# Latent attention with the values stationary, two heads beside each other in the array, and probabilities normalised before they are turned

## The reference

```
q_nope = rms_norm(q[..., :MLA_NOPE], q_nope_norm)
q_pe = apply_rope(rms_norm(q[..., MLA_NOPE:], q_pe_norm), cos, sin)
k_nope = rms_norm(kv[..., :MLA_NOPE], k_nope_norm)
v = kv[..., MLA_NOPE:]
scale = (MLA_NOPE + MLA_ROPE) ** -0.5
...
    s = (einsum('bqhd,bkhd->bhqk', q_nope, k_nope) + einsum('bqhr,bkr->bhqk', q_pe, k_pe)) * scale
    p = softmax(where(causal_mask(s0, Q_BLOCK, L), s, NEG_INF), axis=-1)
    outs.append(einsum('bhqk,bkhd->bqhd', p, v[:, :L]))
o = concatenate(outs, axis=1)
return o.reshape(B, S, H * MLA_V) @ w_o
```

## Time and profile before

| | |
|---|---|
| median of 3 runs | 1319.57 us (1318.76 to 1322.76) |
| profiled execution, its own time | 1321.25 us |
| its span, first to last instruction | 1319.2 us |
| instructions | 15173 |
| mean granted TensorE clock | 0.921 of 2.4 GHz |
| attention of layer 1, part 1 | about 799.6 to 827.7 us |
| attention of layer 1, part 2 | about 852 to 930 us |
| output projection of layer 1 | 930 to 998 us |

### The profile page before, as it was taken

How to read it: one execution, slowest core, us unless ns; L and a number is a source line. 1 busy time by engine, 2 the same in 40 slices (tenths; PEclk the granted TensorE clock), 3 DMA queues, 4 the chain that set the end, 5 groups by cost and what they waited for, 6 DMA issues and landing times.

```text
span 1319.2 us, 15173 instructions
## 1 busy us (share of the span) xinstructions
PE 1054.7 (80%) x5546; PEld 647.5 (49%) x5546; DVE 587.0 (44%) x1466; ACT 329.1 (25%) x912; POOL 107.1 (8%) x119
## 2 busy tenths in 40 slices
PE   2799999988955998777758898899995599777774
PEld 1344444554543665444435456577544366444442
DVE  5999698874354222121122475565235322211111
ACT  2411112763110111111123454354211111111110
POOL 1000000000001212111100000000000121111110
PEclk9999999997965999999968898899996699999997
DMA  9778777014174999999840200200608499999980
GB/s 375 293 303 331 290 262 312 1 73 184 48 308 167 397 400 410 403 407 406 323 174 1 96 1 1 96 1 1 269 35 334 154 398 392 405 407 408 407 317 14
DMA packets 59214, 316.72 MB, mean 240 GB/s; under 512 B 10688, under 2 KB 10944, under 8 KB 27776
## 3 DMA queue, kind: packets, MB, share of 16 engines
q1 hardware_dynamic: 45232, 285.10, 53.0%
q0 software_dynamic: 12752, 27.61, 7.2%
q10 hardware_dynamic: 1152, 2.98, 0.6%
HBM read 308.28 MB, written 25.71 MB: 253 GB/s over the span
## 4 chain that ended last, share of the span: by engine, by line
PE 45%; DMA 26%; DVE 18%; issue 3%; ACT 3%; SPq 3%; DVEq 0%; POOL 0%; POOLq 0%; ACTq 0%
DMA RQK<-in_moe_w 9%; DMA ring<-in_moe_w 9%; PE PP L557 8%; PE PP L622 6%; DMA AHS<-in_moe_w 5%; PE PP L637 5%; PE PP L461 4%; PE PP L480 3%; PE PP L685 3%; DVE AHS L1089 3%; SPq L394 3%; PE PP L522 2%; PE PP L712 2%; DVE ring L1089 2%; PE PP L497 2%
## 5 line engine op out<-in xcount | busy, mean ns | idle before, releaser
L461 PE MATMUL PP<-ring,AHS 128*128 128x512 f32 x384 | 169.9, 599 | 9.3 <-ACT AHS L814 9.3
L1375 DVE TENSOR_TENSOR PS<-PS,PP 128x256 f32<-128x256 f32 x33 | 13.9, 421 | 247.3 <-PE PP L622 247.3
L461 PEld LDWEIGHTS PP<-ring,AHS 128*128 128x128 f32 x384 | 72.5, 192 | 94.8 <-issue 94.8
L557 PE MATMUL PP<-ring,AHS 128*128 128x512 f32 x256 | 113.1, 600 | 0.4 <-ACT AHS L913 0.4
L622 PE MATMUL PP<-RQK,RV 128*64 128x256 f32 x768 | 92.6, 399 | 19.3 <-issue 15.7
L1390 DVE SCALAR_TENSOR_TENSOR PS<-PP,small,GF 128x512 f32<-128x512 f32 x66 | 46.5, 746 | 136.1 <-PE PP L637 136.1
L622 PE MATMUL PP<-ring,RV 128*64 128x256 f32 (+1 forms) x672 | 81.3, 383 | 17.9 <-issue 14.3
L622 PEld LDWEIGHTS PP<-RQK,RV 128*64 128x64 f32 x768 | 66.4, 144 | 48.7 <-issue 33.9
L622 PE MATMUL PP<-AHS,RV 128*64 128x256 f32 x640 | 72.5, 380 | 13.6 <-issue 13.5
L622 PEld LDWEIGHTS PP<-ring,RV 128*64 128x64 f32 (+1 forms) x672 | 61.3, 141 | 41.5 <-issue 23.2
L557 PEld LDWEIGHTS PP<-ring,AHS 128*128 128x128 f32 x256 | 48.7, 193 | 59.1 <-issue 59.1
(11 more groups left out here) (275 smaller groups left out, 1564.3 us busy)
## 6 DMA issues: line engine op xcount, KB each, us to landing
RQK<-in_moe_w SPq DMA_DIRECT2D x72, 1024.0 KB, 29.5
ring<-in_moe_w SPq DMA_DIRECT2D x63, 1024.0 KB, 29.3
AHS<-in_moe_w SPq DMA_DIRECT2D x60, 1024.0 KB, 29.8
ring<-in_ada_t SPq DMA_DIRECT2D x24, 1024.0 KB, 6.6
AHS<-in_ada_t SPq DMA_DIRECT2D x24, 1024.0 KB, 7.1
ring<-in_da_w_qkv SPq DMA_DIRECT2D x12, 1024.0 KB, 9.3
ring<-in_da_w_o SPq DMA_DIRECT2D x4, 1024.0 KB, 11.6
xn_d<-RV POOLq DMA_DIRECT2D x8, 512.0 KB, 2.9
```

What stands on the lines that cost most here:

```text
L461: last = mm(PB[n % 4][:, :], HT[:, c, t * P:(t + 1) * P], us[c // 4][:, (c % 4) * NH:(c % 4 + 1) * NH], start=c == 0, stop=c == C - 1)
L557: last = mm(PB[2 * t + n][:, :], OT[:, k, t * P:(t + 1) * P], us[k // 2][:, (k % 2) * D + n * NH:(k % 2) * D + (n + 1) * NH], start=k == 0 ...
```

## The change

In layer 1's attention, DVE multiplies the probabilities by 1 / `ls` right after the exponentials, in place, and they are turned only after that. The turned probabilities of all four query blocks of a head pair are kept, laid out so that for one block of keys all its later queries are one contiguous run. Once per head pair (`mla_values`) the values of a head become the stationary operand, 128 keys by 64 columns, and up to 512 columns of turned probabilities move; head 0 writes PSUM partitions 0 to 63 and head 1 partitions 64 to 127 of one bank. The result is already turned; ACT copies it to OTM, and the output projection reads it without transposes. The softmax scale moves into the query gain, so DVE's scaling of the maxima and ACT's scale go. The probabilities before turning move from region SCR to region PS (`prm`). On SP's queue the first two units of expert pair 2 wait for `mla_kv` instead of `wo`.

```diff
+TRI_STEP = S - P
+TRI = (T - 1) * TRI_STEP + S
...
+        OTM = view(RH, 0, C, S)
...
+        prm = [view(PS, 1024 * b, 2, S) for b in range(2)]
...
+        def turned(a, t):
+            return SCR[:, TRI * a + t * P:TRI * a + t * P + (t + 1) * TRI_STEP].rearrange(
+                "p (k q) -> p k q", k=t + 1)[:, :, 0:P]
+        def turned_keys(a, k):
+            return SCR[:, TRI * a + k * (TRI_STEP + P):TRI * a + k * TRI_STEP + S]
...
                 if k < 2:
-                    sp.wait_ge(sem("wo"), 2 * T * (l + 1))
+                    sp.wait_ge(*((sem("mla_kv"), 4 * T) if l else (sem("wo"), 2 * T)))
...
+            def mla_turn(i):
+                t, b = i % T, i % 2
+                pe.wait_ge(sem("p"), 32 + i + 1)
+                wait(pe, sem("tev"), i)
+                wait(pe, sem("tev1"), i)
+                for a in range(2):
                     for k in range(t + 1):
-                        last = mm(PB[6 + b][:, 0:P], aT[b][:, 0, k * P:(k + 1) * P], V[:, k, g * P:(g + 1) * P],
-                                  start=k == 0, stop=k == t)
-                else:
+                        last = nc.tensor.transpose(PB[4 + a][:, k * P:(k + 1) * P], prm[b][:, a, k * P:(k + 1) * P], ident[:, :])
+                last.then_inc(sem("tr"), 1)
+
+            def mla_values(g):
+                pe.wait_ge(sem("tev"), 4 * g + 4)
+                pe.wait_ge(sem("tev1"), 4 * g + 4)
+                wait(pe, sem("omla"), g - 1)
+                for k in range(T):
                     for a in range(2):
                         h = 2 * g + a
-                        for k in range(t + 1):
-                            last = mm(PB[6 + b][:, a * VD:(a + 1) * VD], aT[b][:, a, k * P:(k + 1) * P],
-                                      V[:, k, h * VD:(h + 1) * VD], start=k == 0, stop=k == t)
+                        last = mm(PB[6 + g % 2][VD * a:VD * (a + 1), k * P:S], V[:, k, h * VD:(h + 1) * VD], turned_keys(a, k),
+                                  start=k == 0, stop=k == T - 1)
...
                 def turn(t):
-                    if l == 0:
-                        pe.wait_ge(sem("on"), t + 1)
-                    else:
-                        pe.wait_ge(sem("oe"), 64)
+                    if l == 1:
+                        return
...
                 def product(t):
-                    pe.wait_ge(sem("otev"), 4 * l + t + 1)
+                    if l == 0:
+                        pe.wait_ge(sem("otev"), t + 1)
+                    else:
+                        pe.wait_ge(sem("omla"), 8)
...
-                        turn_probabilities(1, i)
-                        if i > i0:
-                            values(1, i - 1)
-                    values(1, i1 - 1)
+                        if i > i0 and i % T == 0:
+                            mla_values(i // T - 1)
+                        mla_turn(i)
+                    mla_values(i1 // T - 1)
...
+                def output(g):
+                    act.wait_ge(sem("av"), 32 + g + 1)
+                    fn(OTM[:, g, :], PB[6 + g % 2][:, :], ACT.Identity).then_inc(sem("omla"), 1)
...
-                    link(red(mx[:, b], PP[pair][:, :, 0:L], AX.X, ALU.max))
-                    ts(nmx[:, b], mx[:, b], -(QK ** -0.5), None, ALU.mult).then_inc(sem("nm"), 1)
+                red(nmx[:, b], PP[pair][:, :, 0:L], AX.X, ALU.max, negate=True).then_inc(sem("nm"), 1)
...
-                    v.reciprocal(rl[:, b], ls[:, b]).then_inc(sem("p"), 1)
+                    link(v.reciprocal(rl[:, b], ls[:, b]))
+                    for a in range(2):
+                        last = ts(prm[b][:, a, 0:L], prm[b][:, a, 0:L], rl[:, b, a:a + 1], None, ALU.mult)
+                    last.then_inc(sem("p"), 1)
...
-                def output(i):
-                    (g, t), b, n = divmod(i, T), i % 2, 32 + i
-                    dve.wait_ge(sem("av"), n + 1)
-                    tt(OTOK[:, t, g * P:(g + 1) * P].rearrange("p (a x) -> p a x", a=2),
-                       PB[6 + b][:, 0:P].rearrange("p (a x) -> p a x", a=2), over(rl[:, b], 2, VD),
-                       ALU.mult).then_inc(sem("oe"), 1)
...
+                ts(qnc, qnc, QK ** -0.5, None, ALU.mult)
```

More of the change, by code:

```diff
@@ L504, in turned_out, with da_turn @@
                 wait(pe, sem("datD"), da_copies(i, False))
[L506 to L509, removed]
-                else:
[L511 to L514, removed]
-                    for k in range(t + 1):
-                        last = mm(PB[6 + b][:, 0:P], aT[b][:, 0, k * P:(k + 1) * P], V[:, k, g * P:(g + 1) * P],
-                                  start=k == 0, stop=k == t)
-                else:
+            def da_turn(i):
+                t, b = i % T, i % 2
+                pe.wait_ge(sem("p"), i + 1)
+                turned_out(i - 2)
+                for k in range(t + 1):
+                    last = nc.tensor.transpose(PB[4 + b][:, k * P:(k + 1) * P], pr[b][:, 0, k * P:(k + 1) * P], ident[:, :])
+                last.then_inc(sem("tr"), 1)
@@ new lines, in da_values @@
+            def da_values(i):
+                (g, t), b = divmod(i, T), i % 2
+                turned_out(i)
+                wait(pe, sem("oe"), i - 1)
+                for k in range(t + 1):
+                    last = mm(PB[6 + b][:, 0:P], aT[b][:, 0, k * P:(k + 1) * P], V[:, k, g * P:(g + 1) * P],
+                              start=k == 0, stop=k == t)
+                last.then_inc(sem("av"), 1)
+            def mla_turn(i):
+                t, b = i % T, i % 2
+                pe.wait_ge(sem("p"), 32 + i + 1)
+                wait(pe, sem("tev"), i)
+                wait(pe, sem("tev1"), i)
+                for a in range(2):
+                    for k in range(t + 1):
+                        last = nc.tensor.transpose(PB[4 + a][:, k * P:(k + 1) * P], prm[b][:, a, k * P:(k + 1) * P], ident[:, :])
+                last.then_inc(sem("tr"), 1)
@@ L866, in exps, with da_turned, mla_turned @@
                 for a in range(2):
-                    last = fn(pr[b][:, a, 0:L], PB[2 * pair + a][:, 0:L], ACT.Exp, bias=nmx[:, b, a:a + 1],
-                              scale=(1.0, QK ** -0.5)[l], accum_out=ls[:, b, a:a + 1])
+                    last = fn((pr, prm)[l][b][:, a, 0:L], PB[2 * pair + a][:, 0:L], ACT.Exp, bias=nmx[:, b, a:a + 1],
+                              accum_out=ls[:, b, a:a + 1])
                 last.then_inc(sem("exp"), 1)
[L871 to L877, removed]
+            def da_turned(i):
+                b, L = i % 2, (i % T + 1) * P
+                act.wait_ge(sem("tr"), i + 1)
+                wait(act, sem("av"), i - 1)
+                fn(aT[b][:, 0, 0:L], PB[4 + b][:, 0:L], ACT.Identity).then_inc(sem("datA"), 1)
+            def mla_turned(i):
+                g, t = divmod(i, T)
+                act.wait_ge(sem("tr"), 32 + i + 1)
+                wait(act, sem("av"), 32 + g if g else 0)
+                fn(turned(0, t), PB[4][:, 0:(t + 1) * P].rearrange("p (k q) -> p k q", k=t + 1),
+                   ACT.Identity).then_inc(sem("tev"), 1)
             def da_attention():
@@ L912, in output_turn @@
                     src = PB[2 * t + half][:, :].rearrange("p (k q) -> p k q", k=4)
-                    last = fn(dst, src, ACT.Identity, scale=subc if l == 0 else 1.0)
+                    last = fn(dst, src, ACT.Identity, scale=subc)
                 last.then_inc(sem("otev"), 1)
@@ L1057, in _ @@
             mla()
-            for t in range(T):
-                output_turn(1, t)
             norm(3)
```

71 lines of the change are left out of this document (27 added, 44 removed).

## The result

The changed kernel takes 1325.84 us (median of 7 runs, 1323.90 to 1326.89) against 1319.57 (median of 7, 1315.88 to 1322.76): a ratio of 1.0045, with a 95% interval of 1.0028 to 1.0061. It is slower by 6.3 us. The forecast was 1320 within a range of 1309 to 1330, with "no change" at 0.50 and "slower" at 0.30. The time lies in the range; the likeliest case did not come true.

A forecast was written before the change was run, and what follows sets the result against it. PE bounds the attention stage now, but after the change a 12.17 us cycle of waits replaces the 12.14 us pair; +3.6, +0.1 and -3.7 sum to 0.0 us, against the 1319.6 median written as 1320, range 1309 to 1330.

The forecast's parts named there:

- part 1: Value products on PE, per head pair: 40 instructions of 4.3 us become 16 taking 2.4, a gain of 1.9.
- Rival B: Value products: the two heads do not overlap in the array; 16 instructions cost 4.3 us, kernel 1335; chance 0.06.
- part 2: DVE per head pair: scalings and outputs go, multiplications come at 0.48 us for 512 columns, 0.42 for 384.
- Rival A: DVE's multiplications run at one column a cycle; the longest cycle of waits grows 0.96 us, kernel 1328; chance 0.17.
- the ring: Steady head pair: longest cycle of waits through PE and DVE (scores, maxima, normalise, copies, transposes, values), 12.17 us against 12.14.
- part 3: Order of work in a steady head pair: PE works 9.7 us, waits the rest; the pair costs the same.
- parts 4 and 5: Ends of attention's two parts, +3.6 us; output projection, transposes gone and an ACT copy in their place, net -3.7.
- the sum of 0.0: Whole kernel: +3.6 at the parts' ends, +0.1 for steady pairs, -3.7 at the output projection, 0.0 us in all.
- Rival D: The clock falls because PE waits a fifth of the time; at half clock 60 us in all; chance 0.02.
- a walk a little too short or long: Kernel time 1324 to 1327, if stepping one head pair through three queues was slightly off; chance 0.05.
- Rival C: Hops overlap better and PE's gain arrives: 1300 if PE's 9.7 us set the pace, 1311 for half; chance 0.20.
- part 6: Items priced at nothing: scale folded into query gain, GpSimd's wait, SP's condition for expert pair 2, copies with strided destination.

The follow-up runs named there:

- heads apart: Changed kernel with the two loops of the value products exchanged (all key blocks of head 0, then head 1): 1334.17 us, 1.0113 of the kernel before.
- the filled kernel: Changed kernel with PE's waits at the parts' ends and before the first product filled with identity products: 1317.45 us, 0.9988 of the kernel before.
- Values spread: Changed kernel with each key block's value products ahead of one step of the next pair: 1311.75 us, 0.9946 of the kernel before.

## Why the prediction was right or wrong

- **Values on PE (part 1).** 2.4 us forecast, 2.31 measured. Right (the four instructions of 512 columns make 0.91 and not the 0.88 of the working, which its sum hides), and "heads apart" shows why: 1.55 us of overlap hang on the order of the two loops. Rival B did not come. The Trainium skill, page "TensorEngine Tiling (Array Packing)", section "Key Properties", says that different tiles can load and multiply in parallel; the trace agrees at 2.31 against 3.86, and adds that the queue's order decides it.
- **DVE's multiplications (part 2).** 0.48 and 0.42 forecast, 0.483 and 0.418 measured. Rival A did not come. The Trainium skill's tier table (page "VectorE: DVE Perf Modes", section "The perf-mode tier table") is borne out for this form: from 128 to 512 columns the cost grows by 0.2 us, 0.52 ns a column. The 0.33 from its cost table (section "The TRN2 errata") was too low. The working also under-rated what that table would do to the ring, which holds four multiplications and not two: an estimate from its 0.33 and 0.26 (for 384 columns) shortens the ring by 0.6 and the sum by 5, not 0.3 and 2. The scalings that went took 0.17 each and not 0.28.
- **The ring (part 3).** 12.17 us forecast, 12.02 measured, with PE's waits where they were forecast, ahead of the transposes of t=2 and t=3. Leaving out the multiplications (10.83), taking most of the values out of the ring (10.99) and lengthening them (13.59) each moved the pair by about what the ring says. That the 1.9 us saved on PE would not arrive was right. DVE is busy 8.0 us a pair, not the 9 that I wrote. The 0.15 between 12.17 and 12.02 is about what the hop from DVE to PE was over-rated by: the ring has it twice at 0.14 (the two times named for it differ by 0.16), and behind the multiplications it was 0.05 and 0.06.
- **The ends and the projection (parts 4 and 5).** At full clock they are near: the filled kernel's parts are 2.5 and 1.4 us longer than before, 3.9 where I had 3.7, though the first part is 0.7 over its 1.8 and the second 0.5 under its 1.9; the first product starts 1.00 behind the last values (0.94 forecast); the products with the transposes gone take 1.83 less (1.75 forecast). That kernel's ratio to before, 0.9988, is the "no change" that the sum of 0.0 stands for. One stretch that the sum does not have differs as well: the projections between the parts are 1.2 shorter than before, where the kernel before runs its last sixteen transposes at half clock and the filled one only a part of them.
- **The step that failed** is part 3's "waits the rest, in pieces under 2 us", taken as free, and with it part 4, which priced the last pair of a part at full clock. Rival D, the clock, was weighed for the whole stage only, from layer 0's average, and given 0.02. What mattered followed from the walk itself: without scores to interleave, the last pair has PE work only between DVE's multiplications. There PE waited 2.06 us, did 0.9 us of transposes, and the clock was at half before the next wait of 1.64 was over. The steady pair, with waits of 1.50 and 0.66 and work for the rest, holds the clock; the last pair does not. Its price is the 8.2 us that filling took away. So the range held the result by its width and not by foresight: 1325.84 lies where the forecast had only 0.05, for a walk a little too short or long, and it was the clock that led there.
- **Rival C** did not come in this order of work. "Values spread" is C made real in part: with one more rearrangement 1.15 of the 1.9 us a pair arrive.
- **SP's queue (part 6)** moved nothing, as forecast.

## What to carry to other kernels

Cheaper work on the bounding engine is worth nothing until the ring of waits around it is walked: here an operand swap that took 2 us of 12 off TensorE brought a DVE operation into the ring and left the pair at the same length. Walk the last round of a pipelined loop by itself, for its waits and for its clock: where the interleaved work runs out, TensorE may fall to half clock and carry it into the stage behind. And where a block of work has to wait for a whole group, see whether its parts can be laid between the steps of the next group.

## What the runs showed of the hardware

- The granted clock fell from 2.4 to 1.2 GHz in a stretch where PE was not once idle for more than 2.06 us: at both ends of a part it was gone behind a wait of 2.06 us and 0.9 us of transposes. With waits of 1.61, 1.20 and 0.61 it held in the profiled run and, by their times, in most but not all. In one execution of the spread kernel waits of 0.79 and 1.27 us held it at the end of part 1 and lost it at the end of part 2, and without the multiplications waits of 1.29 and 0.74 lost it at the end of part 1 and 1.30 and 0.74 held it at the end of part 2: the same waits do not always give the same clock.
- Useless products in these waits made the kernel 8.4 us faster, with 84 more instructions in the queue.
- Two runs of 64-column products in different halves of the array overlap only as neighbours in the queue: 2.31 us against 3.86 for the same 16 instructions.
